# Three column vectors turned on VectorE before they go to DRAM: a two-block transformer kernel on one core

## The chip, the core and the metric

The kernel runs on one core of a Trainium2 chip. It is judged by device time in microseconds (us), the median of 3 runs. TensorE (PE) multiplies matrices, VectorE (DVE), ScalarE (ACT) and GpSimd (POOL) work on rows and columns, and SyncE (SP) issues most of the DMAs. A DMA may also be issued from ACT's own instruction stream, into a queue of its own. Both queues are served by the same 16 DMA engines. SBUF is the memory on the core (128 partitions), PSUM takes the products, and DRAM is the chip's main memory.

## What is computed

256 tokens of width 2048 go through two transformer blocks, all in 32-bit floats. The first has a global and a windowed attention, a squared-ReLU MLP and a gated embedding. The second, cut to what this change touches, is:

```python
mod = silu(c) @ w_mod + b_mod;  sh_m, sc_m, ga_m, sh_f, sc_f, ga_f = split(mod, 6)
lb = cumsum(softmax(hgrn_lb_logits, axis=1), axis=1)[:, 0]       # two rows of 1024
pc = modulate(rms_norm(ctx, g0), shc_m, scc_m) @ w_in[:, :3072]  # the "ctx" product
f = lb + (1 - lb) * sigmoid(pc_f)                                # forget gates
y = gated_merge(conv(...), hgrn(...)) @ w_out
x = x + ga_m * rms_norm(y, norm_post_mix)
m = square(relu(modulate(rms_norm(x, g1), sh_f, sc_f) @ mlp_w1)) @ mlp_w2
x = x + ga_f * rms_norm(m, norm_post_mlp)
```

Three vectors are first made as columns, that is with entry b * 128 + p in partition p, column b: the bound `lb` (2 x 1024), the mixer gate `ga_m * norm_post_mix` (2048) and the MLP gate `ga_f * norm_post_mlp` (2048). They are needed as rows, the same 1024 or 2048 numbers in every partition. To get from one to the other they are written to DRAM as one long row and read back into all partitions.

## The kernel before, in words

Every large product is cut into *pieces*: 256 rows of a weight matrix by 512 columns, 512 KB, in four buffers that take turns. For each piece
- SP waits until DVE is through with the piece four back, then issues the load of `raw` (`load`, L620);
- ACT rounds it to the high part `whi` (`split`, L723) once the load has landed and PE is through with the piece four back;
- DVE subtracts to get the low part `wlo` (L1943);
- PE multiplies: high by high, low by high, high by low, 12 matmuls (L1460).

ACT, DVE and SP each have their instructions written out in a fixed order, and each works strictly in that order. Other work is put between the pieces by hand: a dictionary `extra` says what is done ahead of which slot, where slot u of a stage rounds the piece u + 3 of it. What matters here:

- First stage (`in`): ACT issues `lb_columns_out` (L782) and right behind it `silu_rows_out` (L788), at about 96 us. SP issues at the same time small tables (`bm`, L637).
- Stage `ctx` (from 1068.67 us): slots 5, 8 and 12 of ACT hold `lb_rows_in` (L1010), `gate_column_out(0, 3)` (L1014) and `embedding_in` (L1024, a 2 MB load). Slots 15 and 16 hold the two squares `norm2_square` (L1043), with the copy of PSUM to `cv` (L739) between the chunks; slot 17 holds `norm2_high(0)` (L747), and DVE's slot 18 the low part `hlo` (L1961). PE turns 128 by 128 tiles of `res` between its pieces (L1439); turn number t waits until `hlo` number t - 2 has been made.
- Second MLP (`mlp2`): slot 142 holds `gate_column_out(1, 5)` (L1014) and slot 150 the read `gate_row_in(1, gbc4)` (L1020). Right behind L1014 stands `blocks_in`, four loads `hgather` (L934) of hidden values that DVE turned in 32 by 32 blocks (L2191) and that went through DRAM.

The columns themselves are made by DVE in `lb_softmax` (L1995 to L1998), `other_gains` (L2244) and `last_mods` (L2608).

Of the kernel before, what the change touches and what calls it, by code (L numbers as in the profile page):

```python
# [7 lines left out]
ALU = mybir.AluOpType  # L8
ACT = mybir.ActivationFunctionType
F32 = mybir.dt.float32  # L10
# [4 lines left out]
P = 128  # L15
T = 256
TH = T // P
D = 2048
KT = D // P
# [12 lines left out]
DH = 1024  # L32
# [18 lines left out]
LB0 = COL["hgrn_lb_logits_2"]  # L51
STACK = 4
# [77 lines left out]
def build(nc, I, out):  # L130

    ctx = ExitStack()
    with ctx:
# [9 lines left out]
        def sb(name, shape, dt):  # L143
            size = int(np.prod(shape[1:])) * (1 if dt == I8 else 4)
            t = at(name, shape, dt, cursor[0])
            cursor[0] += size + (-size) % 32
            return t
# [21 lines left out]
        ident = small[:, 0:P]  # L169
        ones = small[:, P:2 * P]  # L170
        cols = sb("cols", [P, NCOL], F32)
        mcol = sb("mcol", [P, 5, KT], F32)
        modT = sb("modT", [P, NMOD * KT], F32)
        modT1 = sb("modT1", [P, 2 * KT], F32)
        lev_at = cursor[0]
# [66 lines left out]
        lb = at("lb", [P, 2, DH], F32, work_at + 48 * K)  # L242
# [40 lines left out]
        hidden_blocks = nc.dram_tensor("hidden_blocks", (P, STACK, TH * STACK * BLK), F32, kind="Internal").ap()  # L283

        scratch = nc.dram_tensor("x_mid", (P, TH, D), F32, kind="Internal").ap()
        row_scratch = nc.dram_tensor("row_columns", (3, D), F32, kind="Internal").ap()
        silu_rows = nc.dram_tensor("silu_rows", (2, D), F32, kind="Internal").ap()
        e_scratch = nc.dram_tensor("e_mid", (P, TH, D), F32, kind="Internal").ap()

# [71 lines left out]
        mcol_done = sem("mcol_done")  # L361
# [4 lines left out]
        lb_out = sem("lb_out")  # L366
        ht_in = sem("ht_in")
        lb_rows = sem("lb_rows")
        lb_soft = sem("lb_soft")
# [57 lines left out]
        gb_done = sem("gb_done")  # L427
        gb_out = sem("gb_out")
# [133 lines left out]
        def col(name, n=KT):  # L562
            return cols[:, COL[name]:COL[name] + n]
# [151 lines left out]
        def _(act):  # L715
# [62 lines left out]

            def lb_columns_out():
                act.wait_ge(lb_soft, 1)  # L780
                for d in range(2):
                    act.dma_start(row_scratch[2, d * DH:(d + 1) * DH].rearrange("(b p) -> p b", p=P), cols[:, LB0 + 16 * d:LB0 + 16 * d + 8],  # L782
                                  allow_slow_non_contiguous=True).then_inc(lb_out, 16)

            def silu_rows_out():
                act.wait_ge(silu_done, 1)
# [4 lines left out]
            def silu_rows_in(phase):  # L791
                if phase:
                    act.wait_ge(m_mul, PHASE_FIRST[phase][1])
                else:
                    act.wait_ge(lb_out, 64)
                for v, h in CROWS_LOADS[phase]:
                    act.dma_start(crows[:, CROWS_HOLD[phase][v, h]], silu_rows[v, h * (D // 2):(h + 1) * (D // 2)].partition_broadcast(P))\
                        .then_inc(crows_in, 16)
# [206 lines left out]
                                        **{d_first + 15 + 2 * g: (lambda g=g: mod_high("normc", g, xhi, mcol[:, 1], modT1[:, 0:KT])) for g in range(8)}}))  # L1005

            def lb_rows_in():
                act.wait_ge(lb_out, 64)
                act.wait_ge(m_mul, n_mlp1_ops)
                act.dma_start(lb[:].rearrange("p d n -> p (d n)"), row_scratch[2].partition_broadcast(P)).then_inc(lb_rows, 16)  # L1010

            def gate_column_out(n, k):
                act.wait_ge(mcol_done, k)
                act.dma_start(row_scratch[n].rearrange("(b p) -> p b", p=P), mcol[:, 3 + n], allow_slow_non_contiguous=True).then_inc(gb_done, 16)  # L1014

            def gate_row_in(n, dst):
                act.wait_ge(gb_done, 16 * n + 16)
                if n == 0:
                    act.wait_ge(on_done, NPAIR)
                act.dma_start(dst[:], row_scratch[n].partition_broadcast(P)).then_inc(gb_out, 16)  # L1020

            def embedding_in():
                act.wait_ge(t_done, TG["normc"][0] + 8)
# [146 lines left out]
            for c in range(14):  # L1170
                col_, g = c % 2 * NCH, g0 + c
                if c < 2:
                    f = evac_to(rows5[:, RV], col_, g)
                elif c < 6:
                    f = forget_out(col_, c, g)
                elif c < 10:
                    f = sig_only(rows5[:, RQ + (c - 6) // 2], col_, g)
                elif c < 12:
                    if c == 10:
                        act.wait_ge(spill, 32)  # L1180
                    f = half_evac(urow, c, g)
                else:
                    f = half_evac(cgrow, c, g, ACT.Sigmoid)
# [745 lines left out]
        def _(dve):  # L1929
            steps = [0]  # L1930

            def step(ins):

                steps[0] += 1
                ins.then_inc(dve_step, 1)
                dve.wait_ge(dve_step, steps[0])
# [48 lines left out]
            l0, l1 = lb_cols[:, 0], lb_cols[:, 1]  # L1985
# [7 lines left out]
            def lb_softmax():  # L1993
                dve.wait_ge(lb_exp, 1)
                step(nc.vector.tensor_tensor(l1, l0, l1, ALU.add))  # L1995
                step(nc.vector.reciprocal(l1, l1))
                step(nc.vector.tensor_tensor(l0, l0, l1, ALU.mult))
                nc.vector.tensor_scalar(l0, l0, 2.0 ** -64, None, ALU.max).then_inc(lb_soft, 1)  # L1998

            def silu_columns():  # L2000
                dve.wait_ge(c_exp, 1)
# [218 lines left out]
            NM, NP, NX = 5 * KT, 4 * KT, 2 * KT  # L2220
# [20 lines left out]

            def other_gains():
                dve.wait_ge(mod_out, 2)
                nc.vector.tensor_tensor(mcol[:, 3], modT[:, 2 * KT:3 * KT], col("norm_post_mix_2"), ALU.mult).then_inc(mcol_done, 1)  # L2244
                dve.wait_ge(mcol_done, 3)

            def norm4_gain():
# [357 lines left out]
            def last_mods():  # L2605
                dve.wait_ge(m_mul, n_ops)
                step(mod_parts(modT[:, NM:], NM, NMOD * KT, bmod[:, NM:]))
                nc.vector.tensor_tensor(mcol[:, 4], modT[:, NM:], col("norm_post_mlp_2"), ALU.mult).then_inc(mcol_done, 1)  # L2608

            def post4_gain(c):  # L2610
                dve.wait_ge(S["sq", "post4"], c + 1)
# [155 lines left out]
```

## Time and profile before

| | us |
|---|---|
| median of 3 runs (2815.36 to 2816.72) | 2815.65 |
| the profiled execution, its own time | 2814.87 |
| the profiled execution, its span | 2813.1 |
| PE busy in that span | 2772.0 (99%) |
| DVE busy | 1959.8 (70%) |
| ACT busy | 1374.8 (49%) |
| mean granted clock of TensorE | 0.996 |

The span lies between the first and the last instruction; the execution's own time is 1.8 us longer. Busy times of different engines overlap. A timeline row tells start, duration, engine, line and operation, and in square brackets how long the engine stood idle before and what released it. A granted clock of 1.00 is TensorE at 2.4 GHz, 0.50 is 1.2 GHz.

### The profile page before, as it was taken

To read this page: it belongs to the slowest core of one execution; us is meant where nothing else is said; L and a number is where in the kernel's file an instruction comes from. 1 tells how busy PE (TensorE), PEld (TensorE's weight loads), DVE (VectorE), ACT (ScalarE), POOL (GpSimd) and SP (SyncE) were. 2 spreads that over 40 slices of the span, in tenths; PEclk is the share of its full clock that TensorE was granted. 3 is DMA by queue.
4 is the path that set the end of the run, shared out by engine and by line. 5 is a ranking of instruction groups with operands and counts; after the bars stand their busy time and mean duration, and the time that the engine had idled before them with its cause. 6 is when DMAs were issued, how large, how long until landed. Compare 5 with 4: busy or idle time off the path is not lost.

```text
span 2813.1 us, 33877 instructions
## 1 busy us (share of the span) xinstructions
PE 2772.0 (99%) x12808; PEld 2302.5 (82%) x12808; DVE 1959.8 (70%) x2280; ACT 1374.8 (49%) x1718; POOL 153.4 (5%) x110
## 2 busy tenths in 40 slices
PE   9999999999999999999999999999989999999998
PEld 7888888888888887788788888898878888878887
DVE  5667777898997675757685488687875467645555
ACT  5446554443444465557444444664554444344443
POOL 0000010010110100000000001000001001010010
PEclk9999999999999999999999999999999999999999
DMA  8963888888888777565666666408857688787674
GB/s 295 210 201 131 280 289 275 276 279 287 301 283 312 254 250 227 193 195 171 206 193 196 201 183 187 142 2 310 311 188 227 198 275 277 257 210 226 204 225 157
DMA packets 312499, 638.80 MB, mean 227 GB/s; under 512 B 34912, under 2 KB 39904, under 8 KB 310496
## 3 DMA queue, kind: packets, MB, share of 16 engines
q1 hardware_dynamic: 295504, 603.61, 67.1%
q10 hardware_dynamic: 16848, 33.22, 3.7%
q8 instruction: 94, 1.54, 0.2%
q14 instruction: 53, 0.43, 0.0%
HBM read 625.69 MB, written 12.00 MB: 227 GB/s over the span
## 4 chain that ended last, share of the span: by engine, by line
PE 93%; DVE 2%; DMA 2%; ACT 1%; issue 1%; ACTq 0%; SPq 0%; DVEq 0%; POOLq 0%; POOL 0%
PE ps L1460 87%; DMA raw<-w_in 1%; PE ps L1439 1%; PE ps L1821 1%; PE ps L1801 1%; PE ps L1620 1%; PE ps L1481 1%; PE ps L1839 1%; DVE wlo L1943 0%; PE ps L1561 0%; PE ps L1541 0%; DMA hgather<-hidden_blocks 0%; ACT whi L723 0%; ACTq L934 0%; DVE cf L2289 0%
## 5 line engine op out<-in xcount | busy, mean ns | idle before, releaser
L1943 DVE TENSOR_TENSOR wlo<-raw,whi 128x1024 fp32r<-128x1024 f32 x940 | 1171.5, 1252 | 756.3 <-ACT whi L723 752.3
L723 ACT ACTIVATE whi<-raw 128x1024 fp32r<-128x1024 f32 x939 | 994.0, 1060 | 1221.5 <-PE ps L1460 1045.9
L1460 PE MATMUL ps<-whi,hhi 128*128 128x512 f32 x2032 | 549.2, 392 | 2.1 <-ACT whi L723 1.9
L1460 PE MATMUL ps<-wlo,hhi 128*128 128x512 f32 x2032 | 543.6, 389 | 1.0 <-DVE wlo L1943 1.0
L1460 PE MATMUL ps<-whi,hlo 128*128 128x512 f32 x2032 | 544.0, 389 | 0.0
L1460 PE MATMUL ps<-whi,xhi 128*128 128x512 f32 x1632 | 442.2, 393 | 6.7 <-ACT whi L723 3.2
L1460 PEld LDWEIGHTS ps<-wlo,hhi 128*128 128x128 f32 x2032 | 381.4, 188 | 81.0 <-DVE wlo L1943 1.4
L1460 PEld LDWEIGHTS ps<-whi,hlo 128*128 128x128 f32 x2032 | 381.1, 188 | 79.5
L1460 PEld LDWEIGHTS ps<-whi,hhi 128*128 128x128 f32 x2032 | 378.6, 188 | 81.2 <-ACT whi L723 2.3
L1460 PE MATMUL ps<-whi,xlo 128*128 128x512 f32 x1632 | 439.5, 391 | 0.1
L1460 PE MATMUL ps<-wlo,xhi 128*128 128x512 f32 x1632 | 438.2, 390 | 0.0
L1460 PEld LDWEIGHTS ps<-whi,xhi 128*128 128x128 f32 x1632 | 304.9, 189 | 71.4 <-ACT whi L723 4.9
L1460 PEld LDWEIGHTS ps<-wlo,xhi 128*128 128x128 f32 x1632 | 307.4, 188 | 64.8 <-DVE wlo L1943 0.2
L1460 PEld LDWEIGHTS ps<-whi,xlo 128*128 128x128 f32 x1632 | 306.6, 188 | 64.2 <-DVE xlo L1972 0.5
L2123 DVE CUSTOM_DVE_ANT_0 mraw<-mraw,crows 128x1024 f32<-128x1024 f32 x192 | 234.4, 1221 | 3.7 <-DMA crows<-silu_rows 1.5
L2685 POOL TENSOR_TENSOR sqrow<-rrow 128x512 f32<-128x512 f32 x64 | 100.6, 1593 | 1139.7 <-ACT rrow L955 1139.7
L2123 DVE CUSTOM_DVE_ANT_0 ps<-mraw,crows 128x1024 f32<-128x1024 f32 x64 | 78.5, 1226 | 4.6 <-DMA crows<-silu_rows 4.6
L2388 DVE SCALAR_TENSOR_TENSOR yT<-uT,cols,yT 128x252 f32<-128x252 f32 (+17 forms) x144 | 52.8, 428 | 0.0
L2660 POOL TENSOR_TENSOR stat<-stat 128x2 f32<-128x2 f32 x9 | 10.3, 1142 | 655.1 <-DVE stat L2133 440.2
L1274 ACT ACTIVATE dec<-ps 128x1024 f32<-128x1024 f32 x32 | 32.5, 1024 | 17.1 <-PE ps L1801 10.8
L1821 PE MATMUL ps<-qD,kD 128*128 128x128 f32 x256 | 34.7, 279 | 3.7 <-DVE qD L2464 2.1
L1821 PEld LDWEIGHTS ps<-qD,kD 128*128 128x128 f32 x256 | 31.0, 191 | 5.1 <-DVE qD L2464 3.1
(301 smaller groups left out, 1517.0 us busy)
## 6 DMA issues: line engine op xcount, KB each, us to landing
raw<-w_in SPq DMA_DIRECT2D x296, 512.0 KB, 4.5
raw<-mlp_w SPq DMA_DIRECT2D x256, 512.0 KB, 4.4
mraw<-w_mod_turned SPq DMA_DIRECT2D x192, 512.0 KB, 6.4
raw<-w_up SPq DMA_DIRECT2D x128, 512.0 KB, 5.1
raw<-w_down SPq DMA_DIRECT2D x128, 512.0 KB, 5.2
raw<-w_o SPq DMA_DIRECT2D x32, 512.0 KB, 5.7
raw<-w_ple_gate SPq DMA_DIRECT2D x32, 512.0 KB, 3.8
raw<-w_out SPq DMA_DIRECT2D x32, 512.0 KB, 5.7
```

The costliest lines, as they stand in the source:

```text
L723: nc.scalar.activation(whi[:, s % NSLOT], raw[:, s % NSLOT], ACT.Copy).then_inc(hi_done, 1)
L1274: nc.scalar.activation(dst, src, ACT.Exp).then_inc(d_done, 1)
L1439: ins = nc.tensor.transpose(ps[:, TB[t % 2], c:c + P], src, ident)
L1460: ins = nc.tensor.matmul(ps[:, bank(par) + th], a[:, kt, th * P:(th + 1) * P], b[:, (s + u) % NSLOT, k], start=(kt == 0 and m == 0), stop= ...
L1481: ins = nc.tensor.matmul(ps[:, bank(g) + th], a[:, kt, th * P:(th + 1) * P], b[:, u % NSLOT, k], start=kt == 0 and m == 0, stop=kt == KT - ...
L1620: ins = nc.tensor.transpose(ps[:, TB[(t0 + h) % 2], a * T + th * P:a * T + (th + 1) * P], sqrow[:, th, f:f + P], ident)
L1801: ins = nc.tensor.matmul(out_of[:, :, 0:4:3] if d == 0 else out_of[:, :, 1:3], w, sums_r[:, m:m + 2].rearrange("p l (r c) -> p l r c", r=2 ...
L1821: ins = nc.tensor.matmul(o[:, (2 * hh + n) * P:(2 * hh + n + 1) * P], k[:, hh, n * P:(n + 1) * P], q[:, hh, t * P:(t + 1) * P], start=True ...
L1943: nc.vector.tensor_tensor(wlo[:, s % NSLOT], raw[:, s % NSLOT], whi[:, s % NSLOT].bitcast(F32), ALU.subtract)\
L2123: nc.vector.tensor_tensor_reduce(out=product, in0=w, in1=crows[:, CROWS_HOLD[phase][v, h]], scale=1.0, scalar=0.0, op0=ALU.mult, op1=ALU.a ...
L2388: nc.vector.scalar_tensor_tensor(out=y, in0=tap_part(uT[:, ct], ct, dd, True), scalar=wcol(TAPS // 2 + dd, ct), in1=y, op0=ALU.mult, op1=A ...
L2685: nc.gpsimd.tensor_tensor(sqrow[:, th], rrow[:, th], rrow[:, th], ALU.mult).then_inc(sq_done, 1)
```

## The change

Each of the three vectors is brought into a form where its values lie side by side. VectorE's block transpose turns each 32 by 32 block of a 128 by 32 tile: afterwards partition 32 * b + k, column j holds what stood in partition 32 * b + j, column k, which is entry k * 128 + b * 32 + j of the vector. So every partition holds 32 neighbours, 128 bytes, and the write to DRAM is 128 runs of 128 bytes. Before, it was one run of 4 bytes for each entry: 1024 for each of two DMAs for the bound, and 2048 for each gate.

The block is 32 columns wide and a gate has 16, so the gate is multiplied twice, into two neighbouring column groups, and the second copy goes to an unread half of a DRAM row that is now 2 x 2048 long. The bound's 32 columns are the bound and a leftover of its softmax. Its read takes two pieces of 1024 out of the row. All three use one tile `cturned`, so DVE waits, ahead of each gate, for the write before it to have landed. Two small tiles grow and shift the buffers behind them by 192 bytes.

```diff
-        mcol = sb("mcol", [P, 5, KT], F32)
+        mcol = sb("mcol", [P, 6, KT], F32)
+        cturned = sb("cturned", [P, 2 * KT], F32)
-        row_scratch = nc.dram_tensor("row_columns", (3, D), F32, kind="Internal").ap()
+        row_scratch = nc.dram_tensor("row_columns", (3, 2 * D), F32, kind="Internal").ap()
             def lb_columns_out():
                 act.wait_ge(lb_soft, 1)
-                for d in range(2):
-                    act.dma_start(row_scratch[2, d * DH:(d + 1) * DH].rearrange("(b p) -> p b", p=P), cols[:, LB0 + 16 * d:LB0 + 16 * d + 8],
-                                  allow_slow_non_contiguous=True).then_inc(lb_out, 16)
+                act.dma_start(row_scratch[2].rearrange("(k b j) -> b k j", b=STACK, j=P // STACK), cturned[:]).then_inc(lb_out, 16)
             def lb_rows_in():
-                act.wait_ge(lb_out, 64)
+                act.wait_ge(lb_out, 48)
                 act.wait_ge(m_mul, n_mlp1_ops)
-                act.dma_start(lb[:].rearrange("p d n -> p (d n)"), row_scratch[2].partition_broadcast(P)).then_inc(lb_rows, 16)
+                act.dma_start(lb[:], row_scratch[2].rearrange("(d n f) -> n d f", d=2, n=2)[0].partition_broadcast(P)).then_inc(lb_rows, 16)
             def gate_column_out(n, k):
                 act.wait_ge(mcol_done, k)
-                act.dma_start(row_scratch[n].rearrange("(b p) -> p b", p=P), mcol[:, 3 + n], allow_slow_non_contiguous=True).then_inc(gb_done, 16)
+                act.dma_start(row_scratch[n].rearrange("(k b j) -> b k j", b=STACK, j=P // STACK), cturned[:]).then_inc(gb_done, 16)
             def gate_row_in(n, dst):
...
-                act.dma_start(dst[:], row_scratch[n].partition_broadcast(P)).then_inc(gb_out, 16)
+                act.dma_start(dst[:], row_scratch[n, 0:D].partition_broadcast(P)).then_inc(gb_out, 16)
                 step(nc.vector.tensor_tensor(l0, l0, l1, ALU.mult))
-                nc.vector.tensor_scalar(l0, l0, 2.0 ** -64, None, ALU.max).then_inc(lb_soft, 1)
+                step(nc.vector.tensor_scalar(l0, l0, 2.0 ** -64, None, ALU.max))
+                nc.vector.transpose(cturned[:], cols[:, LB0:LB0 + 2 * KT]).then_inc(lb_soft, 1)
+            def gate_turned(n, part, gain):
+                twice = lambda v: v.unsqueeze(1).to_broadcast([P, 2, KT])
+                step(nc.vector.tensor_tensor(mcol[:, 3 + n:5 + n], twice(part), twice(gain), ALU.mult))
+                nc.vector.transpose(cturned[:], mcol[:, 3 + n:5 + n].rearrange("p a b -> p (a b)")).then_inc(mcol_done, 1)
             def other_gains():
                 dve.wait_ge(mod_out, 2)
-                nc.vector.tensor_tensor(mcol[:, 3], modT[:, 2 * KT:3 * KT], col("norm_post_mix_2"), ALU.mult).then_inc(mcol_done, 1)
+                dve.wait_ge(lb_out, 48)
+                gate_turned(0, modT[:, 2 * KT:3 * KT], col("norm_post_mix_2"))
             def last_mods():
                 dve.wait_ge(m_mul, n_ops)
                 step(mod_parts(modT[:, NM:], NM, NMOD * KT, bmod[:, NM:]))
-                nc.vector.tensor_tensor(mcol[:, 4], modT[:, NM:], col("norm_post_mlp_2"), ALU.mult).then_inc(mcol_done, 1)
+                dve.wait_ge(gb_done, 16)
+                gate_turned(1, modT[:, NM:], col("norm_post_mlp_2"))
```

In ACT's order nothing moves; only the form of the DMAs changes. This is ACT in the stage `ctx`, slots 6 to 15, before:

```order
L1010 DMA lb<-row_columns 128x2048
L723 ACTIVATE whi<-raw 128x1024 x3
L739 ACTIVATE cv<-ps 128x512 x2
L1014 DMA row_columns<-mcol 128x16x1
L723 ACTIVATE whi<-raw 128x1024 x4
L1024 DMA erow<-e_mid 128x4096
```

and the same place in the changed kernel, whose line numbers are shifted by one:

```order
L1009 DMA lb<-row_columns 128x2x1024
L724 ACTIVATE whi<-raw 128x1024 x3
L740 ACTIVATE cv<-ps 128x512 x2
L1013 DMA row_columns<-cturned 4x32x32
L724 ACTIVATE whi<-raw 128x1024 x4
L1023 DMA erow<-e_mid 128x4096
```

The write of the gate stands where it stood, four pieces ahead of the 2 MB load. On DVE one instruction is added at each of the three places. In the second MLP, where the MLP gate is made, DVE has before:

```order
L2127 TENSOR_TENSOR modT<-msum 128x16
L2128 TENSOR_TENSOR modT<-modT,cols 128x16
L2608 TENSOR_TENSOR mcol<-modT,cols 128x16
L1943 TENSOR_TENSOR wlo<-raw,whi 128x1024
L2191 STREAM_TRANSPOSE hturned<-sqrow 128x4x128 x2
```

and after the change:

```order
L2132 TENSOR_TENSOR modT<-msum 128x16
L2133 TENSOR_TENSOR modT<-modT,cols 128x16
L2002 TENSOR_TENSOR mcol<-modT,cols 128x32
L2003 STREAM_TRANSPOSE cturned<-mcol 128x32
L1942 TENSOR_TENSOR wlo<-raw,whi 128x1024
L2196 STREAM_TRANSPOSE hturned<-sqrow 128x4x128 x2
```

The product is twice as wide and the block transpose stands ahead of the next low part.

## Rows read from the trace of the kernel before

**Rows 1.** The page, part 1.

```profile
PE 2772.0 (99%) x12808; PEld 2302.5 (82%) x12808; DVE 1959.8 (70%) x2280; ACT 1374.8 (49%) x1718; POOL 153.4 (5%) x110
```

**Rows 2.** Timeline of PE: start us, us, operation [idle before <-releaser].

```profile
1101.31 1.07 PE L1460 MATMUL ps<-whi,xhi 128*128 128x512 f32 x4
...
1104.03 1.07 PE L1460 MATMUL ps<-whi,xhi 128*128 128x512 f32 x4
...
1107.22 1.21 PE L1460 MATMUL ps<-whi,xhi 128*128 128x512 f32 x4 [0.31 <-ACT whi L723]
...
1110.12 0.60 PE L1439 MATMUL ps<-small,res 128*128 128x128 f32 x4
...
1113.33 1.07 PE L1460 MATMUL ps<-whi,xhi 128*128 128x512 f32 x4
...
1126.82 1.08 PE L1439 MATMUL ps<-small,res 128*128 128x128 f32 x4 [4.58 <-DVE hlo L1961]
...
1132.82 1.10 PE L1460 MATMUL ps<-whi,xhi 128*128 128x512 f32 x4
...
2499.80 1.20 PE L1460 MATMUL ps<-whi,xhi 128*128 128x512 f32 x4 [2.23 <-ACT whi L723]
...
2508.87 1.20 PE L1460 MATMUL ps<-whi,xhi 128*128 128x512 f32 x4 [0.61 <-ACT whi L723]
```

**Rows 3.** Chain of waits, window 85 to 135 us: start us, us, what.

```profile
84.93 50.09 PE ps L1460 x221
```

**Rows 4.** DMA issues: operation, count, KB each, median us from issue to landing.

```profile
raw<-w_in SPq DMA_DIRECT2D x296, 512.0 KB, 4.5
...
row_columns<-mcol ACTq DMA_DIRECT2D x2, 8.0 KB, 12.5
cols<-gain_columns ACTq DMA_DIRECT2D x1, 8.0 KB, 3.3
```

**Rows 5.** Windows, PE alone: us, PE busy, granted clock, DMA share, GB/s.

```profile
1072.00:1088.00 16.00, 16.00 (x73) 1.00 0.90 332
1091.50:1104.00 12.50, 12.50 (x56) 1.00 0.62 35
1128.00:1132.00 4.00, 4.00 (x11) 0.50 0.83 277
2487.00:2498.00 11.00, 10.58 (x47) 1.00 0.91 80
```

**Rows 6.** Timeline of ACT, stage `ctx`.

```profile
1090.64 0.38 ACTq L1014 DMA_DIRECT2D row_columns<-mcol  x1
...
1106.11 1.06 ACT L723 ACTIVATE whi<-raw 128x1024 fp32r<-128x1024 f32 x1 [8.92 <-DMA raw<-w_in]
1106.12 0.33 ACTq L1024 DMA_DIRECT2D erow<-e_mid  x1
...
1115.25 1.06 ACT L723 ACTIVATE whi<-raw 128x1024 fp32r<-128x1024 f32 x1 [3.96 <-DMA raw<-w_in]
...
1119.06 1.06 ACT L739 ACTIVATE cv<-ps 128x512 f32<-128x512 f32 x2
```

**Rows 7.** Timeline of ACT, stage `mlp2`; the last row is another such gather.

```profile
2487.30 11.29 ACTq L934 DMA_DIRECT2D hgather<-hidden_blocks  x4
2498.70 2.01 ACT L723 ACTIVATE whi<-raw 128x1024 fp32r<-128x1024 f32 x2 [10.84 <-issue]
...
2155.94 1.77 ACTq L934 DMA_DIRECT2D hgather<-hidden_blocks  x4
```

**Rows 8.** Line L2191's instructions (duration ns min/median/max), and DVE's timeline in `mlp2`.

```profile
L2191 DVE STREAM_TRANSPOSE hturned<-sqrow x18: 661/684/705, 2125.6 to 2702.2; 128x512 f32<-128x512 f32 x18
...
2477.61 0.17 DVE L2608 TENSOR_TENSOR mcol<-modT,cols 128x16 f32<-128x16 f32 x1
```

**Rows 9.** Landing of loads of w_in issued 1097 to 1099.5, then 1106 to 1111 us.

```profile
DMA to landing us min/median/max: 12.4/14.3/16.3
...
DMA to landing us min/median/max: 9.0/9.1/9.2
```

More of the change, by code:

```diff
@@ L1007, in lb_rows_in @@
             def lb_rows_in():
-                act.wait_ge(lb_out, 64)
+                act.wait_ge(lb_out, 48)
                 act.wait_ge(m_mul, n_mlp1_ops)
-                act.dma_start(lb[:].rearrange("p d n -> p (d n)"), row_scratch[2].partition_broadcast(P)).then_inc(lb_rows, 16)
+                act.dma_start(lb[:], row_scratch[2].rearrange("(d n f) -> n d f", d=2, n=2)[0].partition_broadcast(P)).then_inc(lb_rows, 16)
             def gate_column_out(n, k):
                 act.wait_ge(mcol_done, k)
-                act.dma_start(row_scratch[n].rearrange("(b p) -> p b", p=P), mcol[:, 3 + n], allow_slow_non_contiguous=True).then_inc(gb_done, 16)
+                act.dma_start(row_scratch[n].rearrange("(k b j) -> b k j", b=STACK, j=P // STACK), cturned[:]).then_inc(gb_done, 16)
             def gate_row_in(n, dst):
```

## The prediction, made before the changed kernel ran

> **What bounds the kernel now.** I read the engines' shares first. PE is busy for 2772.0 of the span's 2813.1 us [rows 1]. So only 41 us of the span are PE standing still, and an edit that leaves the matmuls alone can pay only there, or where the matmuls ran at the lower clock. Next I looked at every place where a DMA of this change is issued, and at PE around it [rows 2, 3].
>
> Around the bound's write (issued at 96 us) the chain is one unbroken stretch of PE from 84.93 us on, for 50.09 us [rows 3]. Nothing is to be won there, whatever the DMAs do.
>
> Around the mixer gate's write PE stops twice: 0.31 us before 1107.22, for `whi`, and 4.58 us before 1126.82, for `hlo`. Around the MLP gate's write it stops for 2.23 us before 2499.80 and 0.61 us before 2508.87, both for `whi` [rows 2].
>
> Then the DMAs. The writes of the gates, 8 KB each, take 12.5 us to land, while a 512 KB weight load takes 4.5 us, and a small load in 128 runs 3.3 us [rows 4]. They also hold back everything else: the DMA engines move 332 GB/s in the 16 us before the first gate's write and 35 GB/s in the 12.5 us behind it; behind the second, 80 GB/s [rows 5]. PE's pieces start 2.72 us apart where nothing is late (1104.03 - 1101.31) [rows 2]; 512 KB in that time ask for about 193 GB/s, so at 35 GB/s the four buffers run dry.
>
> **What that does at the first gate.** The write goes out at 1090.64. One rounding follows, per piece, as soon as PE goes on to the next piece; for the hand-over from PE to ACT I allow an estimated 0.2 to 0.26 us. The one that should run at about 1098.85 (PE goes on at 1101.31 - 2.72 = 1098.59) starts at 1106.11 after 8.92 us of waiting for its load [rows 6]. Number the pieces of the stage so that the one it rounds is piece 14; PE begins it at 1107.22 instead of 1104.03 + 2.72 = 1106.75 [rows 2]. Of these 0.47 us 0.31 is shown as idle; I count the visible 0.31 and below 0.17 for the slower first matmuls after a stop.
>
> The larger loss comes later. ACT stays behind: piece 17 is rounded at 1115.25, again waiting for its load for 3.96 us, because the 2 MB load was also only issued at 1106.12 and now shares the engines [rows 6]. The two squares, the copy at 1119.06 and the first `hhi` follow in ACT's fixed order, and PE's turn gets its `hlo` at 1126.82, 7.76 us after the copy starts [rows 2, 6]. It was due at 1126.82 - 4.58 = 1122.24.
>
> Would this stop be there without the late loads? Take off 0.48 us of PE's delay. The turn is due at 1121.76. The copy needs PE to be through with the chunk. PE starts the next piece at 1113.33 [rows 2], so 1112.85 without the delay; the copy could start a hand-over behind that, at 1113.05, if ACT is not late. 1113.05 + 7.76 = 1120.81, which is 0.95 us before the turn is due. So ACT's order alone does not make the stop; its lateness of 6 us does. The rounding ahead of the copy, of piece 18, would be free to start at 1109.9 (1110.12 - 0.48, and a hand-over), and has until 1112.05: another 2.1 us spare.
>
> What could still be late is that load. The 2 MB load is issued when the rounding of piece 14 starts, so now at about 1098.9 instead of 1106.12. It then meets the loads of pieces 16 to 19. Loads issued just behind it took 9.0 to 9.2 us before [rows 9]. Piece 18's load goes out once piece 14 is done on DVE, at about 1102.7; + 9.1 is 1111.8, inside 1112.05, and by then the 2 MB are nearly gone, so I expect less. Piece 17's load is issued in the same moment as the 2 MB load and is wanted at 1107.0, 8.1 us later; 9.1 us makes it 1 us late, which the 2.1 us spare take. I put the rest of this stop at 0, with 0 to 2.2 us as its bounds (the latter if both are 2 us later than this and nothing absorbs it).
>
> The clock belongs to this stop. After it TensorE is granted 0.50 of its clock, that is 1.2 GHz [rows 5], and the turn and the piece behind it take 1132.82 - 1126.82 = 6.00 us. A turn and a piece at full clock take 3.21 us (1113.33 - 1110.12) [rows 2]. That is 2.8 us. After the stop of 2.23 us at 2499.80 the clock stayed at 1.00, so a rest of up to that size would not bring it back.
>
> **At the second gate.** ACT issues the write and behind it four gathers, which take 11.29 us to issue, where another such set took 1.77 us. ACT sits for 10.84 us in issuing [rows 7], and PE runs out of `whi`. With a write of 128 runs the issue should take 1.8 us again and the roundings fall back on their time. The gather then lands about 10 us earlier, so the 0.61 us, which follow from `hhi` being late, go too. I take both as gone: 2.84 us.
>
> **What the new writes cost.** 2048 runs over 16 engines are 128 each, in 12.5 us, so 98 ns for a run. The new write has 128 runs, 8 on each engine. At the same 98 ns it is 0.8 us; if a run costs by its bytes, 32 times that, it is 25 us and worse than before. The nearest row for 128 short runs is the load of 8 KB at 3.3 us, all included [rows 4]; I go by that, with 0.8 and 25 us as ends. The Trainium skill, DMA: Bandwidth & Descriptors, section Specifications, speaks against the change: it asks for at least 512 bytes for full rate and says that below this the DMA engine does a read-modify-write. By this rule a run of 128 bytes is no better a run than one of 4 bytes; the number of runs falls by 16 all the same, which is the 0.8 us by the rows. No row here shows a write of 128-byte runs by itself.
>
> DVE gets one block transpose at three places, one product twice as wide at two, and one more wait for its own result. A transpose of 128 x 512 takes 684 ns, a small product 0.17 us [rows 8]; so 0.17 us at least and 0.68 at most, and I take 0.2 each. In `mlp2` the next low part stands right behind the product, so it is 0.2 us late, as is the transpose of hidden values behind it. PE uses that low part three pieces later, about 8 us, which hides it. The waits for `lb_out` and for `gb_done` have been met for hundreds of us when DVE gets there. Cost: 0, up to 0.3 us. ACT issues one DMA less. A buffer shift of 192 bytes I put at 0, within 1 us either way, since no row speaks of it.
>
> **Sum, on the profiled execution.** Stops: 0.31 + 4.58 + 2.23 + 0.61 = 7.73 us. Low clock: 2.8. The first four matmuls after a stop take 1.20 where others take 1.07 us, 0.13 to 0.17 each for three of them [rows 2]: 0.45. Together 11.0 us: 2814.87 - 11.0 = 2803.9. The median lies 0.78 us above the profiled execution, so 2804.7.
>
> **Rivals.**
> 1. *The stop at 1122 stays in good part.* The 2 MB load now starts 7.2 us earlier and meets four loads in flight; if piece 17 or 18 lands 4 to 6 us later than I reckon, the turn waits 2 to 4 us, perhaps with the low clock. For it: loads beside the 2 MB took 9 us, twice the usual [rows 9]. Against: the spare 2.1 + 0.95 us. If all 7.4 us stay, the gain is 3.6 us: 2812.1.
> 2. *A short run costs by its bytes, or the 128-byte writes hold the engines as long as the 4-byte ones did.* Then nothing changes but DVE's fractions: 2815.7. For it only the size rule above; against it, that 8 KB in 128 runs landed in 3.3 us.
> 3. *Slower.* The same collision as in 1, but worse than the stop it replaces. To lose, the first place must grow by more than the 3.0 us that the second gives. Stop and clock in it follow piece 17's rounding one for one, so that load would have to land 3 us later than the 1115.2 of now. It was issued at 1098.9, so that is over 19 us of landing; the longest here was 16.3, with the 4-byte writes in the way [rows 9]. With 6 us more than that it is 2818.7.
>
> **Chances.** Forecast, 8 to 12.5 us gained: 72%. Rival 1, 3 to 8 us gained: 17%, half of it over the bound below. Rival 2: 6%. Rival 3: 3%. Something else, 2%. A measurement of this kernel can tell about 0.2%, 5.6 us, from no change; so faster 0.82, same 0.14, slower 0.04. The likeliest case alone spans 2803 to 2807.5. For 8 in 10 I reach to rival 1's end: 2802.5 to 2812.
>
> **What would show it.** Right: the three writes land in 3 to 5 us; throughput stays near 200 GB/s or above behind 1090 and 2487; no `whi` waits 8.92 us; no PE stop before about 1121 and no 0.50 clock behind it; the four gathers issue in about 1.8 us; around 96 us PE does not change. Wrong: a stop of over 2 us left at the turn, with the 2 MB load beside it (the share of the late loads was misjudged); or small writes that still land in over 10 us.

## The result: 2800.84 us, and the profile after

| | before | after |
|---|---|---|
| median of 5 runs each, same chip, us | 2815.65 | 2800.84 |
| lowest to highest | 2814.82 to 2816.72 | 2800.11 to 2801.83 |
| ratio, with 95% interval | | 0.9949 [0.9938, 0.996] |
| the profiled execution | 2814.87 | 2801.83 |
| its span | 2813.1 | 2800.0 |

The change saves 14.8 us. 2804.7 was forecast, with 2802.5 as the low end; the kernel came out 1.7 us below that end. In the profiled executions it is 13.1 us of span.

PE's share of the page, which answers to [rows 1]:

```profile
PE 2768.3 (99%) x12808; PEld 2300.3 (82%) x12808; DVE 1960.7 (70%) x2283; ACT 1375.5 (49%) x1718; POOL 155.4 (6%) x110
```

PE has 3.7 us less busy time (most of it time at the low clock) and 9.4 us less idle time. No matmul was removed. DVE has its three added instructions and 0.9 us more.

PE's timeline of the changed kernel at the places of [rows 2]; start, duration, operation, idle before:

```profile
1106.47 1.07 PE L1459 MATMUL ps<-whi,xhi 128*128 128x512 f32 x4
...
1121.44 0.63 PE L1438 MATMUL ps<-small,res 128*128 128x128 f32 x4 [0.24 <-DVE hlo L1960]
1121.83 1.17 PE L1459 MATMUL ps<-whi,xhi 128*128 128x512 f32 x4
...
1124.66 0.62 PE L1459 MATMUL ps<-whi,xhi 128*128 128x512 f32 x2
...
1341.93 1.19 PE L1459 MATMUL ps<-whi,hhi 128*128 128x512 f32 x4 [0.62 <-ACT whi L724]
```

The stop of 4.58 us at the turn is 0.24 us, and the second piece behind the turn starts at 1124.66, not at 1132.82. At the second gate no stop is left. The last row is one of a place that the prediction did not have. Before, it read:

```profile
1351.39 1.20 PE L1460 MATMUL ps<-whi,hhi 128*128 128x512 f32 x4 [1.86 <-ACT whi L723]
```

It is far from any write of this change; the experiments below come back to it.

The windows, PE alone, as in [rows 5]: us, PE busy, granted clock, DMA share, GB/s.

```profile
1072.00:1088.00 16.00, 16.00 (x72) 1.00 0.88 317
1091.50:1104.00 12.50, 12.50 (x57) 1.00 0.73 238
1128.00:1132.00 4.00, 4.00 (x19) 1.00 0.89 304
2487.00:2498.00 11.00, 11.00 (x50) 1.00 0.69 228
...
2477.50:2488.50 11.00, 11.00 (x50) 1.00 0.84 246
```

Behind the first write the DMA engines moved 35 GB/s and now move 238. Behind the second they moved 80. The second write now goes out 9.56 us earlier, so the stretch right behind it is the last row: 246 GB/s (and 228 in the old stretch). The clock at 1128 is the full one, where it was 0.50.

ACT in `ctx`, against [rows 6]. The write goes out at the same time, and the rounding behind it is no longer held by its load:

```profile
1090.36 0.54 ACTq L1013 DMA_DIRECT2D row_columns<-cturned  x1
...
1098.57 1.06 ACT L724 ACTIVATE whi<-raw 128x1024 fp32r<-128x1024 f32 x1 [1.66 <-PE ps L1459]
1098.60 0.40 ACTq L1023 DMA_DIRECT2D erow<-e_mid  x1
...
1109.86 1.06 ACT L724 ACTIVATE whi<-raw 128x1024 fp32r<-128x1024 f32 x1 [4.79 <-DMA raw<-w_in]
...
1113.67 1.06 ACT L740 ACTIVATE cv<-ps 128x512 f32<-128x512 f32 x2
```

and ACT in `mlp2`, against [rows 7]: the four gathers are issued in 1.88 us, 11.29 before.

```profile
2477.26 0.53 ACTq L1013 DMA_DIRECT2D row_columns<-cturned  x1
2477.89 1.88 ACTq L933 DMA_DIRECT2D hgather<-hidden_blocks  x4
2479.96 1.06 ACT L724 ACTIVATE whi<-raw 128x1024 fp32r<-128x1024 f32 x1 [1.66 <-PE ps L1459]
```

The chain of waits holds the one load that is late:

```profile
1098.67 11.17 DMA raw<-w_in
```

And the new block transpose, all of its gate instances (duration in ns, lowest, median, highest):

```profile
L2003 DVE STREAM_TRANSPOSE cturned<-mcol x2: 211/212/213, 1076.5 to 2468.3; 128x32 f32<-128x32 f32 x2
```

The traces give no landing for these writes. Their packets are in the trace of the changed kernel: the last of the 128 packets of 128 bytes has ended 3.5, 1.5 and 3.4 us after the issue (bound, mixer gate, MLP gate). The landing of about 6 us that an expectation below names is that of reads of the same DRAM rows.

**Ledger of the profiled pair**, by the same piece in both traces. Start of `ctx`: 0.28 us earlier. First gate: the second piece behind the turn is 8.16 us earlier (1132.82 to 1124.66), so 7.9 there. The stop near 1350: from 8.16 to 9.46 us (1351.39 to 1341.93), so 1.3. To the MLP gate's write 0.1 more, 9.56 us. The second gate and its tail: from 9.56 to 13.1 us, so 3.5. The medians differ by another 1.8 us, since the profiled execution of before lay 0.78 us below its median, and that of after 0.99 above.

### The profile page after: what moved, and what is told of

It reads as the page before. It is cut to its first block, busy times and chain, and to the rows that moved or that the text cites. A ratio compares the mean times of both kernels' runs of the same rounds, so it can differ in the third digit from the quotient of the medians.

```text
span 2800.0 us, 33881 instructions
## 1 busy us (share of the span) xinstructions
PE 2768.3 (99%) x12808; PEld 2300.3 (82%) x12808; DVE 1960.7 (70%) x2283; ACT 1375.5 (49%) x1718; POOL 155.4 (6%) x110
## 4 chain that ended last, share of the span: by engine, by line
PE 94%; DVE 2%; DMA 1%; ACT 1%; issue 1%; SPq 0%; DVEq 0%; POOLq 0%; POOL 0%; ACTq 0%
PE ps L1459 87%; DMA raw<-w_in 1%; PE ps L1820 1%; PE ps L1438 1%; PE ps L1800 1%; PE ps L1619 1%; PE ps L1480 1%; PE ps L1838 1%; DVE wlo L1942 1%; PE ps L1560 0%; PE ps L1540 0%; ACT whi L724 0%; DVE cf L2295 0%; PE ps L1674 0%; PE ps L1659 0%
## 5 line engine op out<-in xcount | busy, mean ns | idle before, releaser
L2667 POOL TENSOR_TENSOR stat<-stat 128x2 f32<-128x2 f32 x9 | 10.3, 1140 | 649.8 <-DVE stat L2138 440.0
L1273 ACT ACTIVATE dec<-ps 128x1024 f32<-128x1024 f32 x32 | 32.5, 1024 | 17.2 <-PE ps L1800 10.8
L1800 PE MATMUL ps<-sums_r,rows5r 128*128 128x256 f32 x128 | 33.9, 300 | 1.3 <-ACT dec L1273 1.1
```

Of the source, the lines that this page charges most:

```text
L1273: nc.scalar.activation(dst, src, ACT.Exp).then_inc(d_done, 1)
L1800: ins = nc.tensor.matmul(out_of[:, :, 0:4:3] if d == 0 else out_of[:, :, 1:3], w, sums_r[:, m:m + 2].rearrange("p l (r c) -> p l r c", r=2 ...
```

## The experiments

Each was compared with the kernel before on the same chip. That matters: the kernel before had a median of 2812.4 us in two of these comparisons, 2812.7 in one and 2816.1 in one, where the pair above had 2815.65.

**Which of the three vectors pays?** In each kernel one vector keeps the new form and the others go back to runs of 4 bytes, product and write both. The edit for a vector that goes back:

```diff
-                act.dma_start(row_scratch[n].rearrange("(k b j) -> b k j", b=STACK, j=P // STACK), cturned[:]).then_inc(gb_done, 16)
+                act.dma_start(row_scratch[n, 0:D].rearrange("(b p) -> p b", p=P), mcol[:, 3 + n], allow_slow_non_contiguous=True).then_inc(gb_done, 16)
```

The mixer gate alone in the new form:

> Only the mixer gate goes out turned, in runs of 128 bytes; the bound and the MLP gate keep their 4-byte runs. Theory A (each gate's write pays for its own stops, and the 1.4 us that the later stop at 1340 us lost is a consequence of the mixer gate's place): the span falls by 7.9 us for the stops and the clock at 1107 to 1133 us, and by about 1.4 us more at 1340 us; 9 to 10 us in all, and the stops of 2.23 and 0.61 us at the MLP gate stay. Theory B (the 1.4 us belong to the shifted buffers or to chance between executions): 7.9 us here, and the 1.4 us appear elsewhere.

Measured: 2804.43 us against 2812.41, ratio 0.9975 [0.9964, 0.9985]: 8.0 us. No stop at the turn; at the MLP gate PE still stops:

```profile
2498.39 1.20 PE L1464 MATMUL ps<-whi,xhi 128*128 128x512 f32 x4 [1.61 <-ACT whi L724]
```

The MLP gate alone:

> Only the MLP gate goes out turned; the bound and the mixer gate keep their 4-byte runs. Theory A: 3.1 to 3.5 us less, all of it behind 2484 us; the stops of 0.31, 4.58 and about 1.9 us at 1107, 1126 and 1351 us and the halved clock stay. Theory B (shifted buffers give the 1.4 us at 1340 us): 4.9 us less, with the stop at 1351 us down to 0.6 us.

Measured: 2808.97 us, 0.9989 [0.998, 0.9998]: 3.4 us. The turn has its stop back, and the window behind the first write moves 53 GB/s:

```profile
1125.12 1.08 PE L1443 MATMUL ps<-small,res 128*128 128x128 f32 x4 [4.26 <-DVE hlo L1965]
```

The bound alone:

> Only the bound goes out turned; both gates keep their 4-byte runs. Theory A: no change, within 0.5 us, although the write now lands in about 6 us instead of 13 and the small columns behind it do too, because PE never stops in this stretch. Rival: the late small tables of the first stage cost something later after all, then 1 to 2 us less.

Measured: 2811.27 us, 0.9995 [0.9986, 1.0004], not told from nothing. Its stops are 3.82 us at the turn and 3.36 at the MLP gate.

The two gates give 8.0 + 3.4 = 11.4 us, and each alone takes away the stops at its own place and none at the other gate. That is the division of the prediction, 7.9 and 3.1 (its stops, clock and slower first matmuls).

**Is it the writes, or what DVE and the buffers do now?** Here everything of the change stays, the transposes, the doubled product and the shift by 192 bytes, except that the three writes take the 4-byte form from the old columns.

> All of the change's work on DVE, its waits and its larger buffers, but all three vectors still written in runs of 4 bytes. Theory A: DVE's additions and the buffer shift cost nothing and give nothing, so the time of the kernel before within 0.5 us. Theory B: the buffer shift gives the 1.4 us, so 1.4 us less and a shorter stop at 1351 us. Rival C: DVE's additions cost up to 1 us.

Measured: 2811.99 us, 0.9999 [0.999, 1.0008]. The work on DVE and the shift cost or give nothing that the time can tell, and the gain is in the form of the writes. The traces tell one small thing apart: the 0.3 us ahead of `ctx` are lost in all four profiled executions of the kernel before and in no other kernel here, those with old writes included, so they do not come from the writes.

**The changed kernel once more**, as the level for what follows:

> The changed kernel once more, beside the kernel before on the same chip. If the 14.8 us between the first medians were in part chance between executions of the kernel before, which spread over 7 us (2808.7 to 2815.8) where the changed one spread over 1.7, the difference is smaller here: about 12 us (8.0 + 3.4 + 1.1 of the three parts by themselves). If the parts only add up to the whole together, it is 14 to 15 us again. The stop at 1340 us should again be of another size than 0.6 us.

Measured: 2801.22 us against 2812.42, 0.9959 [0.9945, 0.9973]: 11.2 us, where the first pair gave 14.8. The changed kernel is at the same time as before (2800.84); it is the kernel before that is 3.2 us lower.

**Why was the old write slow?** The prediction had it by the number of runs, 98 ns each (theory A in the expectations). The changed kernel gets one more write behind each gate's write, with 2048 runs as the old gate had, of some tile to a DRAM buffer that nobody reads; only SP waits for them, at the end. N is 1, 32 or 128 values to a run, and each run starts 512 bytes behind the one before (the forms with 32 and 128 values do without the last argument):

```diff
+        probe_rows = nc.dram_tensor("probe_rows", (2, P, 16, P), F32, kind="Internal").ap()
...
+                act.dma_start(probe_rows[n, :, :, 0:N], small[:, 0:N].unsqueeze(1).to_broadcast([P, 16, N]), allow_slow_non_contiguous=True).then_inc(probe_done, 16)
```

> The changed kernel with one more write behind each gate's: 2048 runs of 4 bytes from a constant tile to a scratch tensor that nobody reads. Theory A (the number of short runs makes the loss): the write lands in about 12 us, the stops at the turn (about 4 us, with the clock at half) and at the MLP gate (1.3 to 3.4 us) return, and the time is back at that of the kernel before, within 2 us. Rival (the columns' scattered places in DRAM made it): much less.

> As the one before, but each of the 2048 runs is 128 bytes long (256 KB). Theory A (a run costs 98 ns whatever its size up to this): 12 to 13 us to land, the same stops, the same time as with 4 bytes. Rival B (cost by bytes): 32 times as long, or, if bytes are cheap, about 1 us, as 256 KB at 330 GB/s, and no stops. Rival C (a run below 512 bytes is rewritten as read and write, whatever its length): as theory A here, but not with 512 bytes.

> As the one before, but each of the 2048 runs is 512 bytes long (1 MB). Theory A (98 ns for a run): 12 to 13 us to land and the stops stay. Rival C (only runs below 512 bytes are dear): 3 to 7 us to land, as other transfers of 1 MB do, no stop at the turn of over 0.5 us and none at the MLP gate; the time of the changed kernel within 2 us.

Measured: 2802.92 us, 2803.41 and 2801.73, against 2812.42. None of the three gives the loss back, so A falls. They lie 0.5 to 2.2 us above the changed kernel on the same chip (2801.22), which five or six runs do not tell from nothing. The landing of the first, with 4-byte runs (KB each, median us from issue to landing), then of the second and the third:

```profile
probe_rows<-small ACTq DMA_DIRECT2D x2, 8.0 KB, 7.5
```

```profile
probe_rows<-small ACTq DMA_DIRECT2D x2, 256.0 KB, 6.0
```

```profile
probe_rows<-small ACTq DMA_DIRECT2D x2, 1024.0 KB, 9.2
```

So what differs between the first and the old gate is only where the 2048 words go: 512 bytes apart, and not side by side. The next four kernels vary that and nothing else. First the exact addresses of the old gate, word b * 128 + p from partition p, so that neighbouring words come from neighbouring partitions (theory D of the expectations: neighbours within the same few bytes are what is slow):

```diff
+                act.dma_start(probe_rows[n].rearrange("(b p) -> p b", p=P), small[:, 0:16], allow_slow_non_contiguous=True).then_inc(probe_done, 16)
```

> The changed kernel with one more write behind each gate's: 2048 runs of 4 bytes that go to the places of the kernel before, so that neighbouring partitions, served by 8 to a DMA engine, write neighbouring words of the same 8 KB of DRAM. Theory D (short writes by different engines into the same few lines of DRAM hold each other up): 12 us or more to land, the stops at the turn and the MLP gate are back, about 2811 us. Rival E (what made the loss is something else in the kernel before, such as reading the columns of the gate tile): as with the 2048 runs at places 512 bytes apart, 7 us to land and 2803 us.

Then the same with 64 bytes between neighbours, `rearrange("(b p x) -> p b x", p=P, x=16)[:, :, 0]`:

> As the one before, in the same order, but every 4-byte run gets 64 bytes of DRAM for itself (128 KB in all). Theory D with lines of up to 64 bytes: 7 us to land, no stops, about 2803 us. If the lines that collide are longer than 64 bytes, or if it is the narrow range of addresses, something between this and the time of the old places.

Then words side by side again, but the 16 neighbours all from one partition, `rearrange("(p b) -> p b", p=P)`; the source words are 8 bytes apart, so that no two make one run:

> As the first, 2048 runs of 4 bytes into 8 KB, but partition after partition: the 16 words of a partition lie side by side, so each 64 bytes are written by one DMA engine alone, one word after the other. Theory D (different engines in one line): 7 us, no stops. Theory D2 (any following short writes into one line, by the same engine too): 12 us or more and the stops. Rival F (the narrow range of 8 KB): also 12 us or more and the stops.

And 32 bytes between neighbours (`x=8`):

> As the run with 4-byte runs 64 bytes apart, but 32 bytes apart (64 KB in all), so that two runs share 64 bytes of DRAM. If short writes hold each other up within 64 bytes: a landing above 7.1 us, between 8 and 13, and part of the stops back, 2804 to 2812 us. If it is within 32 bytes: as with 64 bytes apart, 7 us and 2802 us.

Measured, with the window 1091.5 to 1104 us that holds the first of the two writes. The columns are the time against the kernel before on the same chip, the median landing, and what the DMA engines moved:

| 2048 runs of | us | before | ratio | landing us | GB/s |
|---|---|---|---|---|---|
| 4 bytes, side by side, old places | 2815.94 | 2816.10 | 0.9997 [0.9987, 1.0007] | 12.8 | 79 |
| 4 bytes, side by side, one partition | 2823.47 | 2816.10 | 1.0027 [1.0018, 1.0037] | 20.2 | 62 |
| 4 bytes, 32 bytes apart | 2802.04 | 2812.74 | 0.9961 [0.9947, 0.9976] | 7.4 | 259 |
| 4 bytes, 64 bytes apart | 2802.22 | 2816.10 | 0.9953 [0.9936, 0.997] | 7.1 | 239 |
| 4 bytes, 512 bytes apart | 2802.92 | 2812.42 | 0.9967 [0.9955, 0.9979] | 7.5 | 231 |
| 128 bytes, 512 apart | 2803.41 | 2812.42 | 0.9965 [0.9951, 0.9978] | 6.0 | 262 |
| 512 bytes | 2801.73 | 2812.42 | 0.996 [0.9947, 0.9974] | 9.2 | 333 |

The old addresses alone bring the whole loss back: 2815.94 where before is at 2816.10. Its stops are back too (PE's timeline):

```profile
1125.95 1.09 PE L1442 MATMUL ps<-small,res 128*128 128x128 f32 x4 [4.56 <-DVE hlo L1964]
...
2508.37 2.07 PE L1463 MATMUL ps<-whi,xhi 128*128 128x512 f32 x4 [2.68 <-ACT whi L727]
```

and its landing and window, beside those of the kernel whose words are 32 bytes apart:

```profile
probe_rows<-small ACTq DMA_DIRECT2D x2, 8.0 KB, 12.8
...
1091.50:1104.00 12.50, 12.50 (x57) 1.00 0.91 79
```

```profile
probe_rows<-small ACTq DMA_DIRECT2D x2, 8.0 KB, 7.4
...
1091.50:1104.00 12.50, 12.50 (x57) 1.00 0.87 259
```

Neighbours from one partition are not better but the worst of all, with a stop at the MLP gate of

```profile
2518.76 2.07 PE L1463 MATMUL ps<-whi,xhi 128*128 128x512 f32 x4 [10.82 <-ACT whi L727]
```

so it does not need words from different partitions to be slow. One thing goes with the distance here: words side by side also lie within 8 KB in all, those 32 bytes apart within 64 KB. Against the narrow range as the cause stands the new gate's write: 128 runs within 16 KB, and the window behind it moves 238 GB/s. But that is 128 runs and not 2048, so range and distance are not fully parted. Which part of the chip the words wait in is not shown either. The packets of the trace say that it is not the time that an engine spends on a word. Behind the mixer gate's write of the kernel before, all packets of 4 bytes start between 1091.6 and 1092.9 us and take 9 ns at most. What is slow is the traffic behind them: up to 1104 us a load packet of 2 KB takes 450 ns on average and 4980 at most, where the changed kernel has 112 and 1149.

**Is the 2 MB load of any use later?** Rivals 1 and 3 of the prediction rested on its collision with the loads of weights. In the changed kernel it goes out eight slots later:

```diff
-                         5: lb_rows_in, 8: lambda: gate_column_out(0, 3), 12: embedding_in,
+                         5: lb_rows_in, 8: lambda: gate_column_out(0, 3), 20: embedding_in,
```

> The changed kernel with the 2 MB read of the stage ctx issued at slot 20 instead of slot 12, behind the squares and the first turn. Theory A (the rest of the stop, 0.24 to 0.37 us, and the load of piece 17 that lands 11 us after its issue come from this read): that load lands in 4 to 5 us and the stop is gone; 0.4 us less at most, not clear of noise. Rival: the read now meets the 1.3 MB table load of slot 22 and the next turns wait, 1 to 3 us more.

Measured: 2804.33 us, range 2803.9 to 2806.31, against 2816.10; ratio 0.996 [0.9946, 0.9974]. The changed kernel has 2800.84 and 2801.22 us, but on other chips; on this chip its nearest relative, with words 64 bytes apart beside it, has 2802.22. So the loss of 2 to 3 us is seen in the trace rather than in a comparison. The stop of 0.24 us at the old place is gone. But the load now meets another one, a table of sums issued at 1126.63 (ACT's timeline), and a rounding waits for 6.92 us. PE stops for 1.95 us at 1140.30 and for 2.26 us near 1350, both times with the low clock behind it:

```profile
1134.58 1.06 ACT L724 ACTIVATE whi<-raw 128x1024 fp32r<-128x1024 f32 x1 [6.92 <-DMA raw<-w_in]
```

```profile
1140.30 0.63 PE L1438 MATMUL ps<-small,res 128*128 128x128 f32 x4 [1.95 <-DVE hlo L1960]
...
1142.00 1.91 PE L1459 MATMUL ps<-whi,xlo 128*128 128x512 f32 x4
...
1346.22 2.07 PE L1459 MATMUL ps<-whi,hhi 128*128 128x512 f32 x4 [2.26 <-ACT whi L724]
```

So the collision of rivals 1 and 3 exists. With the later load PE loses 3.7 us around 1140 us, stop and clock together; where the kernel has the load it costs 0.24 us of stop. That ACT has time to spare there and not here is the likely reason, and not shown by a run of its own.

**Is one execution of the kernel before like another?** The kernel before, unchanged, profiled three more times:

> The kernel before, unchanged, one more profile. Theory A (the execution I predicted from was a quick one: its stop at the MLP gate left the clock at full): in some of three looks the MLP gate's stop is followed by the halved clock, 2.5 to 3 us dearer, and the stop near 1350 us lies anywhere from 0.4 to 2.6 us. Rival (the stops are the same in each execution, and the difference is something the change does elsewhere): the same 2.23 and 1.86 us and a full clock at the MLP gate in all three.

> The second look at the kernel before; the expectation is that of the first.

> The third look at the kernel before; the expectation is that of the first.

Measured: 2813.53, 2817.98 and 2814.87 us. These are single executions. All three lie above the medians of the other 38 runs of this kernel on the same chip (2812.41 of 30 and 2812.74 of 8), and one lies above the highest of them (2815.76). PE's first stop at each place, in them and in the others (all for `whi` or, at the turn, for `hlo`):

| execution | turn | near 1350 | MLP gate |
|---|---|---|---|
| before, the one predicted from | 4.58 | 1.86 | 2.23 + 0.61, clock 1.00 |
| before, once more (1) | 4.21 | 1.53 | 3.11, half clock |
| before, once more (2) | 4.56 | 2.14 | 3.95, half clock |
| before, once more (3) | 4.49 | 0.60 | 3.65, half clock behind the first matmuls |
| mixer gate alone new | none | 1.91 | 1.61 |
| bound alone new | 3.82 | 0.47 | 3.36, half clock |
| MLP gate alone new | 4.26 | 2.27 | none |
| all but the writes new | 3.90 | 1.45 | 1.29 |
| changed, words at the old places beside | 4.56 | 2.53 | 2.68, half clock |
| changed, words 32 bytes apart beside | none | 1.71 | none |
| changed, first and again | 0.24, 0.37 | 0.62, none | none |

The stop at the turn is in every execution with the old mixer gate write, always with low clock behind it. The one near 1350 comes in all sizes whichever writes there are, so most of its size is chance; that the old writes add a part is neither shown nor ruled out. The one at the MLP gate varies by itself, and in three of four executions of the kernel before the clock fell with it. In the second of the new ones:

```profile
2503.67 1.07 PE L1460 MATMUL ps<-whi,xlo 128*128 128x512 f32 x4
2504.57 1.07 PE L1460 MATMUL ps<-wlo,xhi 128*128 128x512 f32 x4
2509.59 2.08 PE L1460 MATMUL ps<-whi,xhi 128*128 128x512 f32 x4 [3.95 <-ACT whi L723]
2511.47 1.91 PE L1460 MATMUL ps<-whi,xlo 128*128 128x512 f32 x4
2513.18 1.91 PE L1460 MATMUL ps<-wlo,xhi 128*128 128x512 f32 x4
2514.88 1.14 PE L1460 MATMUL ps<-whi,xhi 128*128 128x512 f32 x4
```

The step from one group of four to the next is 0.90 us here at full clock (2503.67 to 2504.57), so the next group was due at 2505.47; it came 4.12 us late. The three groups behind it took 5.29 us instead of 2.72. That is 6.7 us at this gate, where the execution predicted from lost 3.5.

But the mixer gate varies too, and there the execution predicted from was the dearest. Stop and clock together, counted from the starts of the same pieces against the changed kernel:

| execution of the kernel before | mixer gate, us | MLP gate, us | both, us |
|---|---|---|---|
| the one predicted from | 7.9 | 3.5 | 11.4 |
| once more (1) | 5.8 | 6.2 | 12.0 |
| once more (2) | 7.5 | 6.8 | 14.3 |
| once more (3) | 5.9 | 5.6 | 11.5 |

No kernel here beats the changed one by more than the noise. The later load was the one that could have, and it did not.

## Why the prediction was right, and where it failed

The direction and the mechanism held; the size fell short, and the range with it.

- *The writes hold back the loads, and nothing else of the change counts.* Right: 35 to 238 GB/s and 80 to 228 GB/s; with the old writes and the new DVE work the gain is gone.
- *At the bound's write nothing is to be won.* The chain there is again PE from 84.93 us for 50.09 us, and the bound alone could not be told from no change.
- *First gate: 0.31 + 4.58 us of stop, 2.8 of clock.* Right: 7.9 us in the traces, 8.0 in the medians. A rest of 0.24 us stays. The three later executions of the kernel before have 5.8, 7.5 and 5.9 us here, so the exact hit is luck in part.
- *Second gate: 2.84 us, 3.1 with the slower matmuls.* 3.5 us in the pair of traces and 3.4 in the medians of the run with that gate alone, whose interval reaches from 0.6 to 5.6 us.
- *A rest of up to 2.23 us would not bring the low clock back.* Wrong: with the later load 1.2 GHz followed a stop of 1.95 us. It did no harm here, since the rest was 0.24 us.
- *The writes land in 3 to 5 us.* Their landing is not in the traces; their last packets end 1.5 to 3.5 us after the issue.
- *The 2 MB load would make piece 17 1 us late.* It was 2.9 us late (rounded at 1109.86, wanted at 1107.0), since its load took 11.17 us where 9.1 was reckoned. But the spare time was judged well: the copy put at 1113.05 started at 1113.67, and the turn waited 0.24 us. Rival 1 named the right place; its load was 2.1 us slower than reckoned, where it asked for 4 to 6.
- *The four gathers issue in 1.8 us.* 1.88.
- *DVE's additions at 0.2 us each, hidden.* 0.19 to 0.21 us; no wait followed.
- *98 ns for each run, so 128 runs are cheap.* The conclusion was right and the reason wrong, so this part of the forecast was luck. 2048 runs of 4 bytes land in 7.1 to 7.5 us when they lie 32 bytes apart or more and cause none of the stops. With the price per run, two further writes of 2048 runs would have cost the 11 us again; they did not. The old writes were slow because their words lay side by side, 2048 of them within 8 KB.
- *The size rule.* The Trainium skill (DMA: Bandwidth & Descriptors, section Specifications) asks for 512 bytes at least for full rate. Here 2048 runs of 128 bytes landed in 6.0 us and those of 512 bytes in 9.2 us with four times the bytes. So a byte is dearer in the shorter runs, by 2.6 times, which goes the way of the rule; but a short run is not dearer than a long one, and neither write brought back a stop at the two gates.

**The step that failed** is the last one of the sum: "Together 11.0 us: 2814.87 - 11.0 = 2803.9. The median lies 0.78 us above the profiled execution, so 2804.7." It took the two gates of a single execution for all that the change gives, put every other place at nothing, and carried one execution's distance from its median over to the changed kernel.

What the runs showed in its place: 13.1 us in the profiled pair and 14.8 in the medians. The two gates gave 7.9 + 3.5 = 11.4 us, where the forecast had 11.0. Each stop costs about 0.15 us more than its idle time shows, because the end of a group of matmuls is modelled (a group shows 1.07 us and the next starts after 0.91), and 0.39 us stay at the turn. Outside the gates came 0.3 us ahead of `ctx`, 1.3 at the stop near 1350 and 0.1 behind it, which no term had. The last 1.8 us are the medians, which lie further apart than the two profiled executions: 0.78 us above one, 0.99 below the other.

Why the medians lie that far apart stays open. It is no fixed property of the change: four comparisons gave 14.8 and 11.2 us (the changed kernel) and 13.9 and 10.7 (the same with words 64 and 32 bytes apart beside it), and the low end of 2802.5 asks for 13.2. What moves is the kernel with the old writes. It is at 2812.4 to 2812.7 us in three comparisons on two chips and at 2816.1 on a third chip. The two kernels that have all the new work on DVE and still write side by side go with it: 2811.99 on one of the former, 2815.94 on the latter. The changed kernel, alone or with one of the harmless writes beside it, stays at 2800.8 to 2803.4 everywhere. So the old writes cost more in some comparisons than in others. In which stop the difference lies is not shown. The MLP gate's lower clock, which three later executions had and the one predicted from had not, is a candidate. Against it, both gates together cost 11.4 us in the one and 12.0, 14.3 and 11.5 in the others, and on the chip of those three the MLP gate alone gave 3.4 us.

## What to carry to other kernels

When a column is written to DRAM as a row, look at where neighbouring words land rather than at how many descriptors there are. With 2048 writes of 4 bytes side by side in flight the DMA engines moved 35 to 85 GB/s in the 11 to 12.5 us behind them, where the kernels without such writes had 228 to 333. Turning the blocks first removed this. Words 32 bytes apart, tried as an extra write beside the new ones, showed none of it; no gate was written that way. Price such a stall by what starves behind it, and look for ACT's fixed order, since the largest stop came 30 us after the write. And before a stop enters a sum or a range, profile the kernel before more than once: the stop and the clock behind it differed by up to 3.3 us from one execution to the next at one gate and by 2.1 at the other. Whether a kernel without the stops also varies less is not shown. The changed kernel's runs lie within 1.7 and 2.7 us, but they are five each; five of the kernel before lay within 1.9, and five of the changed one with the 512-byte writes beside it within 5.6.

## What the hardware showed that I had not expected

- Writes of single words side by side are slow by their place: 2048 of them landed in 12.8 us (neighbours from different partitions) and 20.2 us (from one partition), against 7.4, 7.1 and 7.5 us at 32, 64 and 512 bytes apart. If it is the distance that decides, and not the range of addresses, the limit lies between 4 and 32 bytes; it was not narrowed down.
- At 512 bytes apart, a write of 2048 runs of 4 bytes and one of 128 bytes each take about the same time, 7.5 and 6.0 us.
- The length of a stop does not tell whether the clock falls. After stops of 1.95 and 2.26 us with the later load the next matmuls ran at 1.2 GHz (1.91 and 2.07 us for four). After 2.53 us, near 1350 in the kernel with words at the old places, they ran at 2.4 GHz:

```profile
1349.78 1.20 PE L1463 MATMUL ps<-whi,hhi 128*128 128x512 f32 x4 [2.53 <-ACT whi L727]
```
